# A third halved pair of lots in four down projections, one plain pair left, and a new order of the small work around them

## The reference, cut to what matters

```
def swiglu(x, w1, w3, w2):
    return (jax.nn.silu(x @ w1) * (x @ w3)) @ w2
...
for l in range(DEPTH):
    x = x + 0.5 * swiglu(rms_norm(x, ffn1_norm[l]), ffn1_w1[l], ffn1_w3[l], ffn1_w2[l])
...
    x = x + merged @ w_out[l]
    x = x + 0.5 * swiglu(rms_norm(x, ffn2_norm[l]), ffn2_w1[l], ffn2_w3[l], ffn2_w2[l])
```

## Time and profile before

| | |
|---|---|
| time, median of 3 runs | 2742.54 us |
| the profiled execution | 2742.97 us, its span 2741.2 us |
| PE (matmul) busy | 2735.9 us, 100% |
| PE weight load busy | 2344.8 us, 86% |
| DVE / ACT / POOL busy | 1927.5 / 1374.6 / 970.2 us (70 / 50 / 35%) |
| granted TensorE clock | 1.0 in the mean (9, that is 90% or more, in every slice) |

### The profile page before, as it was taken

How to read it: one execution, slowest core, us unless ns; L and a number is a source line. 1 busy time by engine, 2 the same in 40 slices (tenths; PEclk the granted TensorE clock), 3 DMA queues, 4 the chain that set the end, 5 groups by cost and what they waited for, 6 DMA issues and landing times.

```text
span 2741.2 us, 42858 instructions
## 1 busy us (share of the span) xinstructions
PE 2735.9 (100%) x16342; PEld 2344.8 (86%) x16342; DVE 1927.5 (70%) x3192; ACT 1374.6 (50%) x2215; POOL 970.2 (35%) x482
## 2 busy tenths in 40 slices
PE   9999999999999999999999999999999999999999
PEld 8898888777788889999998988887777888899998
DVE  7686857885667447888785778578856674588885
ACT  6353444655355446455563534446553653454553
POOL 0134824433343442232121357244333434432331
PEclk9999999999999999999999999999999999999999
DMA  5333583222222223233332335732222222323322
GB/s 171 108 107 117 150 181 109 78 76 70 85 85 85 85 93 101 93 116 105 108 108 93 116 115 156 175 108 78 77 70 80 90 81 89 97 93 104 108 102 100
DMA packets 113262, 285.19 MB, mean 104 GB/s; under 512 B 35632, under 2 KB 45360, under 8 KB 112560
## 3 DMA queue, kind: packets, MB, share of 16 engines
q1 hardware_dynamic: 113072, 282.61, 33.2%
HBM read 268.93 MB, written 9.44 MB: 102 GB/s over the span
## 4 chain that ended last, share of the span: by engine, by line
PE 99%; DVE 0%; DMA 0%; ACT 0%; issue 0%; SPq 0%; ACTq 0%; DVEq 0%
PE bank L653 21%; PE bank L654 21%; PE bank L655 21%; PE bank L702 8%; PE bank L703 8%; PE bank L704 8%; PE bank L679 1%; PE bank L680 1%; PE bank L681 1%; PE bank L1117 1%; PE bank L1136 1%; PE bank L1151 1%; PE bank L886 1%; PE bank L1250 1%; PE bank L1104 0%; PE bank L1309 0%
## 5 line engine op out<-in xcount | busy, mean ns | idle before, releaser
L495 POOL TENSOR_TENSOR w_lo<-raw,w_hi 128x1024 fp32r<-128x1024 f32 x208 | 519.9, 2503 | 872.1 <-ACT w_hi L487 872.1
L653 PE MATMUL bank<-h_hi,w_hi 128*128 128x512 f32 x1504 | 593.3, 395 | 0.5 <-DVE silu_a L2502 0.3
L655 PE MATMUL bank<-h_hi,w_lo 128*128 128x512 f32 x1504 | 585.9, 390 | 0.0
L654 PE MATMUL bank<-h_lo,w_hi 128*128 128x512 f32 x1504 | 585.8, 390 | 0.0
L567 POOL TENSOR_TENSOR w_lo<-raw,w_hi 128x1024 fp32r<-128x1024 f32 (+1 forms) x138 | 253.0, 1854 | 765.7 <-DVE bank L2423 695.3
L487 ACT ACTIVATE w_hi<-raw 128x1024 fp32r<-128x1024 f32 x294 | 309.3, 1056 | 287.6 <-PE bank L655 249.6
L653 PEld LDWEIGHTS bank<-h_hi,w_hi 128*128 128x128 f32 x1504 | 282.3, 188 | 65.7 <-issue 7.1
L655 PEld LDWEIGHTS bank<-h_hi,w_lo 128*128 128x128 f32 x1504 | 282.3, 188 | 59.9
L654 PEld LDWEIGHTS bank<-h_lo,w_hi 128*128 128x128 f32 x1504 | 282.5, 188 | 56.4
L1692 ACT ACTIVATE t_hi<-bank 128x512 fp32r<-128x512 f32 x276 | 162.6, 599 | 207.1 <-DVE bank L2421 61.7
L653 PE MATMUL bank<-g_hi,w_hi 128*128 128x512 f32 x570 | 222.1, 390 | 0.0
(11 more groups left out here) (494 smaller groups left out, 6226.0 us busy)
## 6 DMA issues: line engine op xcount, KB each, us to landing
raw<-in_w_lots SPq DMA_DIRECT2D x478, 512.0 KB, 3.6
s_wd<-s_z SPq DMA_DIRECT2D x8, 512.0 KB, 2.7
s_t<-s_taps SPq DMA_DIRECT2D x16, 256.0 KB, 11.0
da_s<-da_qk SPq DMA_DIRECT2D x16, 256.0 KB, 4.1
x<-in_x SPq DMA_DIRECT2D x8, 256.0 KB, 5.5
raw_k<-in_w_lots SPq DMA_DIRECT2D x8, 256.0 KB, 5.8
s_w_im<-s_wd SPq DMA_DIRECT2D x32, 64.0 KB, 4.2
s_w_re<-s_wd SPq DMA_DIRECT2D x32, 64.0 KB, 3.0
```

Of the source, the lines that this page charges most:

```text
L495: eng.tensor_tensor(w_lo[:, s], raw[:, s], w_hi[:, s].bitcast(f32), SUB).then_inc(S["lo_done"], 1)
L653: pe.matmul(b[:, :], w_hi[:, s, kw], xh[:, k], start=(k == 0), stop=False)
L654: pe.matmul(b[:, :], w_hi[:, s, kw], xl[:, k], start=False, stop=False)
L655: return pe.matmul(b[:, :], w_lo[:, s, kw], xh[:, k], start=False, stop=(k == nk - 1))
```

## The change

`DOWN_LEAD` goes from 2 to 1. Lots 0 and 1 stay plain; pairs (2, 3), (4, 5) and (6, 7) of each site are halved. The lists around it are rewritten:

- DVE no longer makes the low parts of lots 2 and 3 (POOL does, as for every halved pair). It makes the sums of pair (2, 3) at once, with the low part of S1 between the addition and the low part of T4, then S2, S3, S4, `take_y`, and only then `down` of lots 0 and 1, the second of them inside the sums of pair (4, 5).
- ACT leaves lot 3 out of the up stage's end (it needs only half of it now, `high(act, d + 1, 4)`), and rounds S2 between T2 and T4.
- POOL waits, before the low part of lot 4, until the low parts of all four sums of g are done.
- `down_v` of a pair is taken a step earlier for the pairs after the first.

```diff
-DOWN_LEAD = 2
+DOWN_LEAD = 1
...
                         for i in range(DOWN_LEAD, KT // 2):
+                            if i == DOWN_LEAD + 1:
+                                pool.wait_ge(S["c_ones_g_lo"], LOADED + gs_at(which, th, 3))
                             lows_of_pair(n + 2 * i, early=i == DOWN_LEAD + 1)
...
                 round_gs(which, th, S1, g0)
-                round_gs(which, th, S2, g0)
-                high(act, d)
                 round_t(d, T1)
                 round_t(d, T3)
                 high(act, d + 1, 4)
                 round_t(d, T2)
+                round_gs(which, th, S2, g0)
                 round_t(d, T4)
...
                 high(act, n + 2 * J + 2)
-                high(act, n + 2 * J + 3)
+                if not whole:
+                    high(act, n + 2 * J + 3)
...
                 d = n + 2 * DOWN_LEAD
-                for j in range(2, 2 * DOWN_LEAD):
-                    low_of(V, n + j)
+                add_t(d, T1)
+                add_t(d, T3)
+                low_t(d, T1)
+                add_t(d, T2)
+                low_t(d, T3)
+                low_t(d, T2)
+                add_t(d, T4)
                 low_gs(which, th, S1)
+                low_t(d, T4)
                 low_gs(which, th, S2)
-                for j in range(2 * DOWN_LEAD - 2):
-                    down(n, j, 0)
-                weights_t(d)
-                for j in range(2 * DOWN_LEAD - 2, 2 * DOWN_LEAD):
-                    down(n, j, 0)
                 low_gs(which, th, S3)
                 low_gs(which, th, S4)
                 take_y(d, 0)
+                down(n, 0, 0)
                 for a in range(d, n + KT, 2):
                     i = a - n
+                    if a == d + 2:
+                        down_v(a - 2, i - 2)
                     if a > d:
-                        down_v(a - 2, i - 2)
                         down_w(a - 2, i - 2)
                     add_t(a + 2, T1)
                     add_t(a + 2, T3)
+                    if a == d:
+                        down(n, 1, 0)
                     low_t(a + 2, T1)
...
                     if a > d:
                         down_x(a - 2, i - 2)
                         second_of_v(i)
-                    if a == n + KT - 2:
                         down_v(a, i)
                     low_t(a + 2, T4)
```

## The result

The changed kernel takes 2759.93 us (median of four, 2758.78 to 2761.83) against 2742.51 of the kernel before on the same chip: ratio 1.0064, interval 1.0047 to 1.0081. It is slower, by about what was forecast (2759.3). The profiled execution took 2759.3 us, 2757.4 of it span, 16.2 above the span of before. Of the 36 executions of the kernel before that stand beside the experiments, one took 4537.69 us at a mean granted clock of 0.556 and is left out of every comparison.

The account below looks back on a forecast made before the run. PE, busy 100% of the span, was taken as the bound. Per site, holes 4.67 plus restarts 0.66 less 1.12 saved give +4.21; four sites add 16.8 to 2742.97, 2759.8; the median standing 0.4 lower, forecast 2759.3, range 2751 to 2766.

Parts of the forecast that it names:

- The saving: On PE, a halved pair costs 10.02 us against 10.90 plain: 0.88 a site, 1.12 if the existing hole closes too.
- old hole: PE's one hole among the halved matmuls of the kernel before: 0.24 us a site with the late matmul behind it.
- The cost of a site: Net change at each of four sites: holes 4.67 plus restarts 0.66, less 1.12 saved, +4.21 us.
- restarts: The matmul after each PE hole comes late: six of 0.11 us, 0.66 a site; bounds between nothing and 0.11 each.
- Turn-taking: When DVE and POOL instructions both have two SBUF inputs, the second waits; DVE's first addition of (4, 5) over 2 us.
- Without turns: Rival: DVE and POOL run beside each other at the sites; holes with restarts 3.4, +2.3 a site, 2751.9 us; 9%.
- The point of release: Between DVE and POOL, the second's work seems to start 0.13 us before the first's recorded end.
- What is hidden: `down_v`'s move, lot 3 leaving ACT's list and the loads cost nothing; the first two 0.3 to 0.9 each if uncovered.
- The hold: POOL's new wait before lot 4's low part: without it holes move, their sum staying within 0.3 us a site.
- The clock: Rival: after 2.5 us holes PE's clock halves for one to two products a site; 2765 to 2771 us; 7%.
- main case: The laid-out holes at all four sites, with DVE and POOL taking turns: 2755 to 2764 us, 77%.
- The cover rival: Rival: S1's low parts and `copy_x` come in time, so PE's holes are gone: 2738.0 us; 2%.

Follow-up runs that it names:

- f: Kernel before, with copy_x of the last pair moved ahead of the rounding of the next lot on ACT: 2741.97 us, ratio 0.9997.
- e5: e4 with more DVE and ACT work for pair (2, 3) moved into idle time at the up stage's end, other steps earlier: 2739.05 us, ratio 0.9988.
- e2: Changed kernel with only half of POOL's low part of lot 4 made, old contents read for the rest: 2759.13 us, ratio 1.0056.
- e1: Changed kernel without POOL's new wait before the low part of lot 4: 2761.56 us, ratio 1.0067.
- e4: Changed kernel with lists reordered: copy_x and pair (4, 5)'s sums earlier, POOL's lot 4 waiting for S3's low parts: 2745.41 us, ratio 1.0009.
- g: Changed kernel with copy_x of a pair moved ahead of the rounding of the next lot on ACT: 2758.03 us, ratio 1.0057.
- h: The changed kernel run again unaltered, to see its spread: five executions from 2758.91 to 2760.73 us, median 2759.07.
- e3: Changed kernel with DVE and ACT lists back in the order of before, third halved pair kept, no POOL hold: 2762.89 us, ratio 1.0073.

## Why the prediction was right, step by step

- *Where it is bound.* Right. All of the loss is holes in PE's row, at four sites that agree within 0.09 us.
- *The saving.* Right: 0.88 from 168 matmuls at 0.119, now seen twice. Site 1 of f, which has no old hole, is 41.87, or 41.82 without its one late matmul; less 0.88 it is 40.94. e5's site 1 has 0.24 of holes and is 41.20; the changed kernel's has 5.24 and is 46.20: both are 40.96 without them. The term for the old hole was 0.24, and its removal alone gave 0.14 to 0.21, since f's late matmul takes 0.05 back.
- *The cost of a site* was put at 4.21 and is 4.13. By holes, forecast against measured: first product 0.06 and 0.07; S1 1.01 and 1.09; S2 0.40 and 0.43; `take_y` 0.04 and under 0.03; POOL's lot 4 0.65 and 0.58; `copy_x` 2.51 and 2.50. The restarts were mis-sized: six of 0.11 forecast, 0.66; measured 0.10, 0.07, 0.08, 0.10, 0.11 and 0.11, 0.57. After the holes of S1 and S2 the second matmul is 0.07 or 0.08 late, not 0.11. (The last step of the sum has a slip of 0.1: 2759.8 less 0.4 is 2759.4.)
- *Turn-taking* was the step I was least sure of. It stands, by four rows: the addition of 2.17, the same at 1.08 with POOL's instruction halved (e2), S2's low parts at 3.29 where POOL comes earlier (e1), and POOL's own turn in e4. Without turns 2751.9 us was due. The point of release is close to 0.13 before the recorded end: POOL's 1137.26 and the addition's 1137.81 are 0.55 apart, and 0.69 - 0.13 is 0.56. The Trainium skill ("SBUF — State Buffer", section "A bandwidth-pool intuition that's wrong") gives a release about 115 ns after the holder's end, with DVE as the holder; by that the addition would have ended at 1138.07. In e4 DVE is the holder: its addition's record ends at 1133.74, and POOL's 2.39 us of work at 1136.00, so it started at 1133.61, 0.13 before that end again. The traces decide for the earlier point, whichever engine holds.
- *What is hidden.* The move of `down_v`, lot 3 off ACT's list and the loads were put at nothing, and no wait of PE falls on them; no run took one of them back by itself. `take_y` of pair (4, 5) did lie just under cover; I never laid it out, and it cost nothing only as long as the `copy_x` hole stood before it (g).
- *The hold.* I put it within 0.3 a site; it is worth 0.37, a little more than that.
- *The clock.* I gave it 7% as a rival with one or two slow products at every site, 2765 to 2771. It is real, but happens at some sites of some executions: none in the first profile, one in the second. So it isn't the rival's time but the spread of the main case, 2758.8 to 2761.8 against 0.3 us of the kernel before beside it. The two executions with a mean granted clock of 1.000 took 2758.78 and 2759.30, the two with 0.999 took 2760.55 and 2761.83; the median of 2759.93 is 0.6 above the forecast for that reason, and no other is visible. The main case had no term for this: that its bounds held it is owed to their width, and two small misses, holes and restarts 0.3 us too high in all and the clock left out, pulled in opposite directions. The Trainium skill ("TensorE: Matmul & The Clock Gate", section "What's actually happening") gives idling as what brings back the lower level. Here it did so only sometimes, at 8 of 20 sites with a hole of 2.1 us or more.
- *The cover rival* (2738.0) was unreachable for the change as written. With its conditions met on purpose, e5 comes to 2739.05.

## What to carry to other kernels

Where one engine's row has no holes, price a change as a saving per instruction and, separately, as cover taken from the other engines' work: here the saving was 0.9 us a site and the cover lost 11, and the lists behind it could not be ready. The cure was not to save less but to bring forward, in each engine's list, the steps that PE waits for, past those that nobody is waiting for, and to do as much as can be done in idle time before the stage. When a hole is closed, look for what was late behind it, since its cover is gone too. And where PE waits for DVE and not for POOL, put an instruction with two SBUF inputs on DVE ahead of POOL's long ones: the one that comes second waits for the rest of the other.

## What the runs showed of the hardware

- Low-clock stretches. In 20 sites of five profiled executions with a hole of 2.1 us or more (after, h, e1, e2, e3) there were 8; in 20 sites with none above 1.6 (before, e4, f, g, e5) there were none. The holes before them were 2.1 to 2.9 us. The mean granted clocks of all executions, traced or not, agree with this in the main: below 1.000 in 16 of 21 of the first group, in none of 38 of e4, f, g and e5. But one of the 35 executions of the kernel before beside the experiments took 2745.15 us at 0.999, and it has no trace: so long holes go with such stretches, but that one is needed is not shown. What decides between a hole that is followed by one and a hole of the same length that isn't stays open.
- A low-clock stretch costs 1.4 us in h and about 1.5 in e2, but nothing in e3 (47.04 and 47.01 with, 47.05 and 46.98 without) and 0 to 0.3 in e1. In those two a later hole takes it up: in e1 `copy_x` made PE wait up to 1.6 where the clock had stayed up, and only 0.3 at the first site, where it had not. A slower PE has a cost only if it isn't about to wait anyway.
- Halving one instruction on POOL shortens the record of a DVE instruction that meets it from 2.17 to 1.08 us, though the edit touches nothing on DVE. In a profile such a delay stands as busy time, and no list of waits names it.
